# Two chunked recurrences without the last chunk's state update, its key transposes, copies and decays

## What is computed

```python
def step(state, xs):                       # gated delta rule, one chunk
    u_c, w_c, q_c, k_c, attn_c, last_c = xs
    v_new = u_c - einsum('bhck,bhkv->bhcv', w_c, state)
    o = einsum('bhck,bhkv->bhcv', q_c, state) + einsum('bhij,bhjv->bhiv', attn_c, v_new)
    state = state * last_c[..., None, None] + einsum('bhck,bhcv->bhkv', k_c, v_new)
    return state, o
...
_, o = lax.scan(step, state0, xs)          # the last state is dropped

    # mLSTM, the end of its step
    c_mat = s_keep * c_mat + einsum('bhc,bhck,bhcv->bhkv', w_end, k_c, v_c)
    n_vec = s_keep * n_vec + einsum('bhc,bhck->bhk', w_end, k_c)
    return (c_mat, n_vec, m_new), h_c
_, hs = lax.scan(step, carry0, xs)         # here too
```

## Time and profile before

| | us |
|---|---|
| median of 3 runs | 1982.02 (1980.75 to 1982.06) |
| the profiled execution, device time | 1976.49 |
| its span, first to last instruction | 1974.8 |
| TensorE busy | 1883.6 (95%) |
| TensorE weight loads busy | 1689.1 (86%) |
| VectorE busy | 1077.0 (55%) |
| ScalarE busy | 871.2 (44%) |
| GpSimd busy | 110.6 (6%) |
| mean granted TensorE clock | 0.983 of full |
| mean DMA rate | 92 GB/s |

### The profile page before, as it was taken

One profiled execution on the slowest core, in us unless ns is written; L12 is line 12 of the kernel. 1 busy time (PEld: TensorE's weight loads), 2 busy tenths in 40 slices (PEclk: granted clock), 3 DMA queues, 4 the chain that ended last, 5 costly groups with the idle time before them and its releaser, 6 DMA issues. The chain is left out here.

```text
span 1974.8 us, 31477 instructions
## 1 busy us (share of the span) xinstructions
PE 1883.6 (95%) x12756; PEld 1689.1 (86%) x12756; DVE 1077.0 (55%) x1786; ACT 871.2 (44%) x1437; POOL 110.6 (6%) x140
## 2 busy tenths in 40 slices
PE   7999999999799999999989998999999998999988
PEld 6999999899589999999989976778888885787766
DVE  6666689976643344444452278434444446862343
ACT  6557763667632433332234256343323233424442
POOL 0001140000000000000000020000000002000101
PEclk9999999999999999999999998999999999999989
DMA  7233462255342223222312233223232232321101
GB/s 179 84 92 108 129 191 68 61 166 169 99 120 85 86 92 101 85 85 86 102 49 90 84 69 102 65 86 107 85 101 90 92 99 66 108 65 43 54 12 43
DMA packets 211359, 182.58 MB, mean 92 GB/s; under 512 B 42736, under 2 KB 182000, under 8 KB 211240
## 3 DMA queue, kind: packets, MB, share of 16 engines
q1 hardware_dynamic: 211240, 180.93, 30.9%
HBM read 165.73 MB, written 15.16 MB: 92 GB/s over the span
## 5 line engine op out<-in xcount | busy, mean ns | idle before, releaser
L163 DVE TENSOR_TENSOR main_wlo<-raw,main_whi 128x2048 fp32r<-128x2048 f32 x106 | 244.0, 2302 | 334.4 <-ACT main_whi L156 334.4
L156 ACT CAST main_whi<-raw 128x2048 fp32r<-128x2048 f32 x106 | 201.7, 1903 | 408.1 <-PE ps L178 408.1
L178 PE MATMUL ps<-ffn_xhi,main_whi 128*128 128x264 f32 (+1 forms) x768 | 206.6, 323 | 6.6 <-DVE ffn_xlo L648 6.6
L178 PE MATMUL ps<-ffn_xhi,main_wlo 128*128 128x264 f32 (+1 forms) x768 | 206.6, 324 | 0.0
L178 PE MATMUL ps<-ffn_xlo,main_whi 128*128 128x264 f32 (+1 forms) x768 | 206.5, 323 | 0.0
L178 PE MATMUL ps<-ffn_ahi,main_wlo 128*128 128x264 f32 (+1 forms) x768 | 205.2, 322 | 0.0
L178 PE MATMUL ps<-ffn_alo,main_whi 128*128 128x264 f32 (+1 forms) x768 | 205.0, 321 | 0.0
L178 PE MATMUL ps<-ffn_ahi,main_whi 128*128 128x264 f32 (+1 forms) x768 | 203.9, 320 | 0.0
L178 PE MATMUL ps<-gdn_xhi,gdnf_whi 128*128 128x264 f32 x768 | 161.4, 291 | 4.4 <-DVE gdn_xlo L519 4.4
L178 PE MATMUL ps<-gdn_xlo,gdnf_whi 128*128 128x264 f32 x768 | 156.7, 285 | 0.0
L178 PE MATMUL ps<-gdn_xhi,gdnf_wlo 128*128 128x264 f32 x768 | 156.6, 285 | 0.0
(11 more groups left out here) (498 smaller groups left out, 3701.5 us busy)
## 6 DMA issues: line engine op xcount, KB each, us to landing
raw<-in_ff_up_dram SPq DMA_DIRECT2D x32, 1024.0 KB, 5.4
raw<-in_ff_down_dram SPq DMA_DIRECT2D x32, 1024.0 KB, 5.0
raw<-in_gdn_in_dram SPq DMA_DIRECT2D x24, 1024.0 KB, 5.7
raw<-in_w_in_dram SPq DMA_DIRECT2D x14, 1024.0 KB, 5.3
raw<-in_mlstm_in_dram SPq DMA_DIRECT2D x12, 1024.0 KB, 5.3
raw<-in_gdn_out_dram SPq DMA_DIRECT2D x8, 1024.0 KB, 6.8
gdn_v_spilled<-gdn_o SPq DMA_DIRECT2D x16, 264.0 KB, 2.2
gdn_z_spilled<-gdn_o SPq DMA_DIRECT2D x16, 264.0 KB, 3.7
```

The costliest lines, as they stand in the source:

```text
L156: k.nc.scalar.copy(k.whi[:, slot % SPLIT_SLOTS, :], k.raw[:, slot, :]).then_inc(k.hi_done, 1)
L163: eng.tensor_tensor(k.wlo[:, s, :], k.raw[:, slot, :], k.whi[:, s, :].bitcast(F32), ALU.subtract).then_inc(k.lo_done, 1)
L178: mm = pe.matmul(ps[:, b, 0:k.width], w, x[:, half], start=first and n == 0, stop=last and n == 2)
```

## The change

A flag `carried(u)` is true for every unit whose state a later chunk reads, false for the last chunk's four. Where it is false, the key transposes, the copies of keys and of the last decay column, the decayed new values (or weighted keys), the update matmul and the state addition are left out. Waits that counted on them now count on something that is still there: `new_values` waits for `new_done` instead of `dec_done`; in the mLSTM the value copy waits for `num_ready` instead of `su_ready`, and `turn` for `v_done` instead of `k_done`. The signal that a unit's values are turned moves from the key transpose to the last value transpose.

```diff
@@ gdn_back
+        carried = lambda u: u < NU - NG
@@ tensor
-                for h in range(2):
-                    mm = pe.transpose(ab[0:n, 2 + h, :], key(c, 2 * i + h), k.ident[:, :])
-                mm.then_inc(s.kt_ready, 1)
+                if carried(u):
+                    for h in range(2):
+                        mm = pe.transpose(ab[0:n, 2 + h, :], key(c, 2 * i + h), k.ident[:, :])
+                    mm.then_inc(s.kt_ready, 1)
...
+                elif carried(u - 1):
+                    pe.wait_ge(s.dec_done, u)
                 else:
-                    pe.wait_ge(s.dec_done, u)
+                    pe.wait_ge(s.new_done, u)
...
-                    update(u - 2)
+                    if carried(u - 2):
+                        update(u - 2)
                     output(u - 2)
@@ scalar
-                act.wait_ge(s.kt_ready, u + 1)
-                if u >= NG:
-                    act.wait_ge(s.su_ready, u - NG + 1)
-                nc.scalar.copy(kt[0:n, i, :, :], ab[0:n, 2:4, :]).then_inc(s.kt_done, 1)
+                if carried(u):
+                    act.wait_ge(s.kt_ready, u + 1)
+                    if u >= NG:
+                        act.wait_ge(s.su_ready, u - NG + 1)
+                    nc.scalar.copy(kt[0:n, i, :, :], ab[0:n, 2:4, :]).then_inc(s.kt_done, 1)
@@ vector
-                dve.tensor_copy(kd[0:n, c % 2, head(i)].unsqueeze(2), dt[0:n, i, :, n - 1:n]).then_inc(s.kd_done, 1)
-                dve.wait_ge(s.kd_done, u + 1)
+                if carried(u):
+                    dve.tensor_copy(kd[0:n, c % 2, head(i)].unsqueeze(2), dt[0:n, i, :, n - 1:n]).then_inc(s.kd_done, 1)
+                    dve.wait_ge(s.kd_done, u + 1)
+                    dve.wait_ge(s.kt_done, u + 1)
                 dve.wait_ge(s.kq_ready, u + 1)
-                dve.wait_ge(s.kt_done, u + 1)
...
-                if real(u - 3):
+                if real(u - 3) and carried(u - 3):
                     states(u - 3)
...
-                if real(u - 1):
+                if real(u - 1) and carried(u - 1):
                     decayed(u - 1)
@@ mlstm_mix
+        carried = lambda u: u < MU - MP
@@ scalar
-                if u >= 2:
+                if u >= 2 and carried(u - 2):
                     act.wait_ge(s.su_ready, u - 1)
+                elif u >= 2:
+                    act.wait_ge(s.num_ready, u - 1 - MP)
@@ vector
-                dve.tensor_copy(we[0:n, u % 2, :].unsqueeze(2), w[0:n, b, :, n - 1:n]).then_inc(s.we_done, 1)
+                if carried(u):
+                    dve.tensor_copy(we[0:n, u % 2, :].unsqueeze(2), w[0:n, b, :, n - 1:n]).then_inc(s.we_done, 1)
...
-                if 0 <= t < MU:
+                if 0 <= t < MU and carried(t):
                     state(t)
                 if 0 <= t + 1 < MU:
                     intra(t + 1)
-                    keys(t + 1)
+                    if carried(t + 1):
+                        keys(t + 1)
@@ tensor
-                if u >= 1:
+                if u >= 1 and carried(u - 1):
                     pe.wait_ge(s.k_done, u)
+                elif u >= 1:
+                    pe.wait_ge(s.v_done, u)
...
                 for o in range(2):
-                    pe.transpose(bank_t[0:n, o * P:(o + 1) * P], vf[:, 2 * p + o, t:t + n], k.ident[:, :])
-                mm = pe.transpose(bank_t[0:n, 2 * P:3 * P], qk[:, MP + p, t:t + n], k.ident[:, :])
+                    mm = pe.transpose(bank_t[0:n, o * P:(o + 1) * P], vf[:, 2 * p + o, t:t + n], k.ident[:, :])
+                if carried(u):
+                    mm = pe.transpose(bank_t[0:n, 2 * P:3 * P], qk[:, MP + p, t:t + n], k.ident[:, :])
...
-                if 0 <= t < MU:
+                if 0 <= t < MU and carried(t):
                     update(t)
```

More of the change, by code:

```diff
@@ L2729, in intra @@
                 dve.wait_ge(s.w_exp, 2 * u + 2)
-                dve.tensor_copy(we[0:n, u % 2, :].unsqueeze(2), w[0:n, b, :, n - 1:n]).then_inc(s.we_done, 1)
+                if carried(u):
+                    dve.tensor_copy(we[0:n, u % 2, :].unsqueeze(2), w[0:n, b, :, n - 1:n]).then_inc(s.we_done, 1)
                 if full(u):
-                    dve.wait_ge(s.we_done, u + 1)
+                    if carried(u):
+                        dve.wait_ge(s.we_done, u + 1)
                     dve.wait_ge(s.gram, u - MP + 1)
```

## The result

The changed kernel took 1970.37 us (median of 8 runs, 1966.53 to 1975.5), the kernel before 1981.82 (8 runs, 1979.46 to 1985.19) on the same chip. The ratio is 0.9949, with a 95% interval of 0.9937 to 0.9961: 0.5% faster. The forecast was 1971.9, its range 1967.5 to 1977.5.

A forecast was written before the change was run, and what follows sets the result against it. TensorE was taken as the bound, but in delta rule slots 16 to 18 a ring of update, output and state addition. Delta rule 7.9 + mLSTM 2.2 = 10.1; 1982.0 - 10.1 = 1971.9 us, range 1967.5 to 1977.5.

The forecast's parts named there:

- The ring is what bounded slots 16 to 18: Delta rule, slots 16 to 18: update, output and state addition wait for each other without overlap, 4.3 us a unit.
- Slots 14 and 15 give 1.44: Delta rule: key transposes give 0.44 us, unit 12's update some 1.0, so `close6` of slot 15 comes 1.44 earlier.
- Outputs 13 and 14 stand right behind: Delta rule, slots 16 and 17: both outputs directly follow the new values, at 487.5 and 490.25, the latter with 0.15 slack.
- One new wait of about 0.7: Delta rule's end: TensorE's last output waits 0.6 to 0.7 us for ScalarE's copy of output 14, sharing one bank.
- The transposes of slots 12 and 13 give nothing: Delta rule: their savings stand ahead of a point set by VectorE's DMA; taken at nothing, at most 0.44 us.
- The table load takes 1.28 us and nothing behind it: Delta rule, ScalarE before the copy of output 13: load of 1.28 us, without the 1.38 drain of the skill page.
- The rival that the load holds ScalarE longer: Delta rule: a load of twice its 1.28 us would gain 1.15 us less, giving 1973.05 us; chance 4%.
- mLSTM 2.2: mLSTM, us gained: 0.2 up to step 17, 1.26 in steps 17 and 18, 0.44 in 19, 0.3 at 20.
- The stage before the barrier is not held by SyncE or by the gates: Delta rule's end: gate stores land at about 491, at worst 494.2, under 495.5.
- The clock falls elsewhere: Rival: TensorE's clock falls move with idle time, up to 1.7 us each; 1975.3 or 1968.5 us; chance 12%, half each way.
- The slower case: Rival: clock at 1.2 GHz in the head of the stage after the delta rule, 16 us lost, 1988 us; chance 3%.
- The signs of being wrong: TensorE waits in slots 16 or 17, step 17's waiting goes into step 18, or stages after either place change time.

The follow-up runs named there:

- e3: Kernel before, with only VectorE's state additions of the delta rule's last chunk and the waits for them left out; 1974.44 us, ratio 0.9955.
- e1: Kernel before with the change in the delta rule alone, the mLSTM as before; 1973.99 us, ratio 0.9964.
- e5: Changed kernel with the last delta rule unit's output in the PSUM bank the updates used; 1969.23 us, ratio 0.9939 against the kernel before.
- e2: Kernel before with the change in the mLSTM alone, the delta rule as before; 1980.01 us, ratio 0.9996.
- e4: Changed kernel with the delta rule's last-chunk key transposes and their copies put back; one execution, 1971.21 us.
- e6: Changed kernel with SyncE issuing values and decay rows ahead of the gate stores and loads; one execution, 1969.15 us.
- e7: Changed kernel with the edits of e5 and e6 together; 1969.24 us, ratio 0.9945 against the kernel before.
- e8: e7 plus eleven matmuls whose result nothing reads, in TensorE's gap behind the mLSTM; 1968.82 us, ratio 0.9929 against the kernel before.

## Why the prediction was right

The sum was 7.9 + 2.2 = 10.1; the stretches gave 7.63 + 1.94 = 9.57. The timed medians moved by 11.45 (7.7 to 12.5 by the interval of the ratio), the profiled pair by 9.12. The interval holds 10.1 and 9.57 alike, so the times do not test the parts; the stretches do. What the medians show beyond 9.57 is placed by no trace. By the steps:

- **The ring is what bounded slots 16 to 18.** Shown by e3: without the state additions TensorE has no idle row there.
- **Slots 14 and 15 give 1.44.** It was 1.33: `close6` came at 485.31, and 486.34 + 0.30 - 485.31 = 1.33. The term that was off is the update of unit 12, priced at its start-to-start of 1.00. From L1921 to the second pair of the output it was 1.82 before (482.86 to 484.68) and is 0.93 now (482.73 to 483.66), so it gave 0.89: without the update the first pair takes 0.33 to the next instead of 0.22. ScalarE was called level with TensorE, and was a little ahead of it, since L2026 still stands 0.71 behind L1931.
- **Outputs 13 and 14 stand right behind.** Right for 13, and all but right for 14, whose slack of 0.15 was used up: the copy of output 13 ran from 489.90 to 490.49, and output 14 started at 490.63, 1.04 after L1870 instead of the 0.95 of the walk. That is 0.14 behind the copy's end, as output 15 is 0.15 behind that of the copy it waits for (493.27, 493.42).
- **One new wait of about 0.7.** It is 0.77, and the last output came 2.79 after the one before, against the 2.65 of the walk (490.25 to 492.9). With the 0.09 of the line above and some 0.05 in the last output and its copy this makes 0.28, all that is missing from the 7.9 (L1870 of unit 15, at 489.59, was where the walk had it, 489.3 + 0.30; the 0.11 lost in slot 15 had been made up by a shorter slot 16, 2.68 instead of 2.8, which is luck).
- **The transposes of slots 12 and 13 give nothing.** Right in the changed kernel and in e1, where TensorE waits 0.34 and 0.50 behind the late rows, and for the reason given. It is not a property of the kernel: in e5, with the same order of DMAs, they gave their 0.44.
- **The table load takes 1.28 us and nothing behind it.** The load at 488.61 ends at 489.89 and the next copy starts at 489.90. The rival that the load holds ScalarE longer is out. The Trainium skill, ScalarE: Activation LUTs, section What ACT_TABLE_LOAD costs, has a drain of about 1.38 us with each switch to a different set. Neither this row nor that of the earlier trace rows shows one.
- **mLSTM 2.2.** It was 1.94: 0.12 up to step 17 (forecast 0.2), 0.48 and 0.45 in steps 17 and 18 (0.63 each), and 0.89 from step 19 on (0.44 + 0.3). The first term that was off is the update. It was priced by its own row at 0.53, start to next start. What it takes out of a step is the difference with and without it: L2823, L2832 and L2804 took 0.45 + 0.53 = 0.98 before, L2839 and L2819 now stand 0.54 apart, so 0.44. The second is the ring of VectorE and ScalarE, which was said to get over 1 us shorter a step and not to take over. VectorE's weights came every 3.62 and 3.72 us before (1205.60, 1209.22, 1212.94) and come every 3.42 and 3.41 now (1199.36, 1202.78, 1206.19), because they wait for ScalarE's value copy. TensorE's step 17 is 3.42 as well, so the ring is level with it, at a cost of about 0.1 in step 18. The 0.89 is luck in part: in step 19 the update gave 0.21 instead of 0.44, since the transposes of `back` now wait there, and the wait of step 20 went whole and gave 0.68 instead of 0.3. The wait at step 17, 1.51, was forecast at 1.4.
- **The stage before the barrier is not held by SyncE or by the gates.** Right: the next square starts 0.29 after the last copy.
- **The clock falls elsewhere.** This rival came true and decided nothing, which is luck as well. In four parts of the program outside the two stretches the second trace is 1.2 longer, 0.6 and 2.8 shorter and 2.3 longer, and this nearly cancels. The slower case (a head at 1.2 GHz throughout) did not come: in the head behind the delta rule the clock was at 1.2 GHz for about 3.4 us in both traces, and its new place cost 0.98 of the 1.2.
- **The signs of being wrong.** The prediction named three, and all three showed in small: output 14 stood some 0.1 late behind a copy, the wait at step 17 reached step 18, and the stage behind the delta rule took 0.98 longer. None changed what bounds the two stretches.

## What to carry to other kernels

The tail of a pipeline, where the filling work has run out, is bounded by the ring of dependences between engines: measure its period (4.3 us a unit here) and look which member can go, even if it is an operation of 1.1 us on an engine that mostly waits there. Price a removed instruction by the group with and without it, not by its own start-to-start (0.89 for 1.00 and 0.44 for 0.53 here); where its engine waits behind it, walk forward to see what waits next (here one output bank, 1.0 us more once the last output had another). Edits worth 1 or 2 us in a kernel of 2000 are judged by the distance between two fixed instructions in the trace, since whole runs differ by more.

## What was not expected of the hardware

The spread of the times goes with the granted clock. Of the 8 runs after, the four with a mean clock of 0.981 or 0.982 took 1966.53 to 1968.65 us, the four with 0.977 to 0.980 took 1972.09 to 1975.5. In the 20 runs of before the tie is looser: 1976.3 to 1979.9 from 0.981 on, 1978.63 to 1985.45 below.

Which idle gaps bring the clock down changes between kernels: the same head, with the same 5.13 us wait at L633, took 11.98 us at full clock (after, and within 0.01 e2, e4, e5, e6 and e7) and 13.4 to 14.75 with a fall (before, e1, e3 and e8). The first three that fell are the three without the mLSTM part of the change, and the six that held all have it. So the mLSTM part may be worth 1.4 to 2.8 us more than its stretch, by where it puts the clock's fall. Against it stands e2, where its timed gain is 0.9 us and at most 3.2 by the interval. With one trace of each kernel this is open, and so is whether the filler of e8, which kept the clock at 2.4 GHz at one gap, caused the fall at the next. It would take executions of one kernel traced several times to tell, and these were not made.
